# Gate rows through device memory, and the first expert's rows gathered by selection products

## What is computed

```python
sh1, sc1, gt1, sh2, sc2, gt2 = _adaln(cond, w_mod[l], b_mod[l])     # per layer and group
x = x + gt1 * mix(_modulate(x, norm_g[l, 0], sh1, sc1))             # gate 0 (layer 0), gate 2 (layer 1)
h = _modulate(x, norm_g[l, 1], sh2, sc2)
x = x + gt2 * channel_mixer(h)                                      # gate 1 (layer 0), gate 3 (layer 1)
# channel mixer of layer 0: (silu(h @ wg) * (h @ wu)) @ wd, D_FF = 3584
# channel mixer of layer 1:
top_v, top_i = lax.top_k(h @ w_router, 2)
gates = sum(one_hot(top_i) * softmax(top_v))
for e in range(8):
    out = out + gates[..., e:e+1] * _swiglu(h, w_gate[e], w_up[e], w_down[e])
```

## Time and profile before

| | us |
|---|---|
| median of 3 runs (lowest, highest) | 1557.11 (1556.25, 1558.7) |
| profiled execution, its own time | 1554.79 |
| profiled execution, span from first to last instruction | 1553.0 |
| PE busy | 1435.9 (92%) |
| DVE, ACT, POOL busy | 341.5, 313.6, 114.0 |
| mean granted PE clock, of full speed | 0.966 |
| moved by DMA | 497.66 MB, mean 320 GB/s |

### The profile page before, as it was taken

How to read it: one execution, slowest core, us unless ns; L and a number is a source line. 1 busy time by engine, 2 the same in 40 slices (tenths; PEclk the granted TensorE clock), 3 DMA queues, 4 the chain that set the end, 5 groups by cost and what they waited for, 6 DMA issues and landing times.

```text
span 1553.0 us, 27293 instructions
## 1 busy us (share of the span) xinstructions
PE 1435.9 (92%) x12271; PEld 747.2 (48%) x12271; DVE 341.5 (22%) x413; ACT 313.6 (20%) x386; POOL 114.0 (7%) x171
## 2 busy tenths in 40 slices
PE   4998879989999997699999999999999999999963
PEld 1995659767888864233333333333233333333321
DVE  1434782555454444000000000000000000000004
ACT  2435324353343433001000000000000000000001
POOL 4001153341000002000000000000000000000010
PEclk9899989999999998799999999999999999999997
DMA  8757768645555539577999999999999999999994
GB/s 341 247 193 281 271 254 342 229 138 164 190 189 188 189 126 423 208 266 287 352 365 423 424 407 394 382 354 424 423 402 425 422 397 423 424 398 423 423 422 184
DMA packets 124366, 497.66 MB, mean 320 GB/s; under 512 B 10564, under 2 KB 14336, under 8 KB 102752
## 3 DMA queue, kind: packets, MB, share of 16 engines
q1 hardware_dynamic: 110608, 472.51, 77.8%
q10 hardware_dynamic: 12208, 18.26, 3.2%
q0 software_dynamic: 1440, 5.24, 0.9%
HBM read 476.19 MB, written 19.79 MB: 319 GB/s over the span
## 4 chain that ended last, share of the span: by engine, by line
PE 81%; DMA 6%; DVE 4%; SPq 4%; issue 3%; ACT 1%; POOL 0%; ACTq 0%; POOLq 0%; DVEq 0%
PE ps L1951 32%; PE ps L1999 14%; PE ps L368 6%; PE ps L370 6%; PE ps L369 6%; PE ps L1513 4%; DMA ring_a<-in_moe_down 3%; SPq L492 2%; PE ps L1994 2%; PE ps L1715 1%; PE ps L1581 1%; PE ps L1582 1%; PE ps L1583 1%; PE ps L1726 1%; DMA rows_io<-htok,slot 1%
## 5 line engine op out<-in xcount | busy, mean ns | idle before, releaser
L1951 PE MATMUL ps<-ring_a,hTf 128*32 128x512 f32 (+1 forms) x2336 | 230.7, 546 | 3.5 <-DMA ring_a<-in_moe_up 2.1
L1478 DVE TENSOR_TENSOR diag<-gate_bc,ps 128x512 f32<-128x512 f32 (+1 forms) x46 | 28.5, 621 | 875.3 <-PE ps L1951 873.8
L1951 PE MATMUL ps<-raw,hTf 128*32 128x512 f32 (+1 forms) x2080 | 202.8, 541 | 3.8 <-DMA raw<-in_moe_up 3.2
L340 DVE TENSOR_TENSOR w_lo<-raw,w_hi 128x2048 fp32r<-128x2048 f32 x60 | 137.3, 2301 | 155.7 <-ACT w_hi L336 155.7
L1951 PE MATMUL ps<-ring_b,hTf 128*32 128x512 f32 (+1 forms) x1472 | 145.2, 540 | 2.4 <-DMA ring_b<-in_moe_up 2.4
L1951 PEld LDWEIGHTS ps<-ring_a,hTf 128*32 128x32 f32 x2336 | 73.8, 110 | 144.6 <-issue 136.2
L336 ACT ACTIVATE w_hi<-raw 128x2048 fp32r<-128x2048 f32 x60 | 114.0, 1913 | 124.2 <-PE ps L370 124.2
L1951 PEld LDWEIGHTS ps<-raw,hTf 128*32 128x32 f32 x2080 | 65.9, 110 | 125.3 <-issue 118.6
L368 PE MATMUL ps<-w_hi,hTh 128*128 128x512 f32 x288 | 114.9, 399 | 7.9 <-ACT gate_bc L915 5.6
L370 PE MATMUL ps<-w_lo,hTh 128*128 128x512 f32 x288 | 113.6, 394 | 0.0
L369 PE MATMUL ps<-w_hi,hTl 128*128 128x512 f32 x288 | 113.4, 394 | 0.0
(11 more groups left out here) (340 smaller groups left out, 1569.5 us busy)
## 6 DMA issues: line engine op xcount, KB each, us to landing
raw<-in_w_mod SPq DMA_DIRECT2D x48, 1024.0 KB, 7.6
raw<-in_moe_down SPq DMA_DIRECT2D x23, 2048.0 KB, 25.6
ring_a<-in_moe_down SPq DMA_DIRECT2D x19, 2048.0 KB, 23.5
ring_a<-in_moe_gate SPq DMA_DIRECT2D x14, 2048.0 KB, 21.1
ring_b<-in_moe_down SPq DMA_DIRECT2D x14, 2048.0 KB, 24.8
raw<-in_moe_up SPq DMA_DIRECT2D x12, 2048.0 KB, 23.7
ring_a<-in_moe_up SPq DMA_DIRECT2D x12, 2048.0 KB, 24.0
raw<-in_moe_gate SPq DMA_DIRECT2D x10, 2048.0 KB, 14.6
```

The lines of the kernel that those rows point to most:

```text
L340: nc.vector.tensor_tensor(w_lo[:, w % SPLIT], raw[:, slot % RAW], w_hi[:, w % SPLIT].bitcast(F32), ALU.subtract).then_inc(s["lo_ready"], 1)
L1951: last = MM(ps[TOK * j:TOK * j + TOK, part % 4, 0:w], hTf1[:, kt, q * P + TOK * g:q * P + TOK * g + TOK], wt[:, kt % 2, j, :], start=kt == ...
```

## The change

It does two things.

First, the gates. PE turns the gate columns of `mcol` (or `pgate`) into eight rows of 128 (`turn_gates`, two turns for a gate), ACT copies them to a small tile `grow` (`save_gates`), POOL stores them to device memory (`gate_rows`, `store_gates`), waits until they have landed, and then loads each gate row back with every partition reading the same 4 KB (`fetch_gate`: two transfers of 512 KB for each gate). DVE now waits for the landing (`gate_a`, `gate_b`) where it waited for ACT's copy. The products with ones, the `diag` tiles and the big copies are gone.

Second, the first expert. DVE builds for each group a selection matrix, `sel[token, place] = 1` where the token's place in expert 0's list is `place` (`select`). PE multiplies `htok` with it (`gather`: 16 products of 128 x 128), which leaves the gathered rows already turned; ACT copies them as before (`save_rows`). The load of these rows, and the wait of SP for the scatter in front of it, are gone; the scatter itself stays, and SP waits for it in front of the second expert's rows. `gather(p + 1)`, `select` and `save_rows(p + 1, 0)` for a next pass are at the end of each pass and run in the only pass too. `save_tokens(1)` moves ahead of the exponential. The early picks go to two halves of a ring buffer, the late ones to `tmp` and `xrow`.

The diff, without the list of semaphores, paddings and the waits that only follow from them:

```diff
...
+gate_rows = nc.dram_tensor("gate_rows", (4, NB, D), F32, kind="Internal").ap()
...
+grow = sbuf(tail, "grow", [4, P])
...
-diag = sbuf(tail, "diag", [4, 4, P])
-iota = sbuf(tail, "iota", [N_EXP])
+hm = sbuf(tail, "hm", [4, 512])
+iota = sbuf(tail, "iota", [P])
...
+sel = sbuf(tail, "sel", [NB, P])
...
-picked = (htok, spare[:, 0:2])
-late = (spare[:, 2], spare[:, 3])
+picked = (spare[:, 0:2], spare[:, 2:4])
+late = (flat2(tmp), xrow[:, :])
...
-        if p == 0 and i == 0:
+        if p == 0 and i == 1:
             sp.wait_ge(s["rows_sent"], 64)
-        else:
-            sp.wait_ge(s["xg_turned"], N_EXP * p + i)
+        sp.wait_ge(s["xg_turned"], N_EXP * p + i)
...
             ff_loads(p, i, "U0", e)
-            if i == 0:
-                row_load(p, 0, e)
             ff_loads(p, i, "G1", e)
...
-    def gates(i):
-        if i == 0:
-            pool.wait_ge(s["vnew_turned"], 4)
-        else:
-            pool.wait_ge(s["gates_turned"], i + 1)
-        if i == 2:
-            pool.wait_ge(s["pgate_ready"], 1)
-        else:
-            pool.wait_ge(s["mod_cols_saved"], (2, 3, 4, 6)[i])
-        gate = pgate if i == 2 else mcol[:, i // 2, 24 * (i % 2) + 16:24 * (i % 2) + 24]
-        for h in range(2):
-            for b in range(NB):
-                nc.gpsimd.tensor_tensor(diag[:, 2 * h + b], rep(ident[:, :], 1, 4),
-                                        rep(gate[:, 4 * h:4 * h + 4, b], 2, P), ALU.mult)\
-                    .then_inc(s["diag_ready"], 1)
-    gates(0)
+    def store_gates(n, first, count):
+        pool.wait_ge(s["gate_rows_saved"], n)
+        cut = slice(2 * (first % 2), 2 * (first % 2) + 2 * count)
+        pool.dma_start(gate_rows[first:first + count].rearrange("i b (t p) -> t (i b) p", p=P), grow[0:KT, cut])\
+            .then_inc(s["gate_rows_stored"], 16)
+        pool.wait_ge(s["gate_rows_stored"], 16 * n)
+    def fetch_gate(i):
+        for b in range(NB):
+            pool.dma_start(gate_bc[:, i % 2, b], gate_rows[i, b].partition_broadcast(P))\
+                .then_inc(s["gate_b" if i % 2 else "gate_a"], 16)
+    store_gates(1, 0, 2)
+    pool.wait_ge(s["qs_turned"], 1)
+    fetch_gate(0)
+    pool.wait_ge(s["rows_cleared"], 16)
+    fetch_gate(1)
     pool.wait_ge(s["y_turned"], 2)
     nc.gpsimd.memset(w_rt[:, :, :], 0.0).then_inc(s["band_ready"], 1)
-    gates(1)
...
-    nc.gpsimd.iota(iota[:, :], pattern=[[1, N_EXP]], base=0, channel_multiplier=0,
+    nc.gpsimd.iota(iota[:, :], pattern=[[1, P]], base=0, channel_multiplier=0,
...
-    gates(2)
-    gates(3)
+    store_gates(2, 2, 1)
+    pool.wait_ge(s["x_updated"], 2)
+    fetch_gate(2)
...
                                          htok[:, b], None).then_inc(s["rows_sent"], 16)
+    store_gates(3, 3, 1)
+    pool.wait_ge(s["x_updated"], 4)
+    fetch_gate(3)
...
+    def save_gates(n, bank, first, count):
+        act.wait_ge(s["gate_rows_turned"], n)
+        if n > 1:
+            act.wait_ge(s["gate_rows_stored"], 16 * (n - 1))
+        cut = slice(2 * (first % 2), 2 * (first % 2) + 2 * count)
+        nc.scalar.activation(grow[0:KT, cut].rearrange("p a n -> p (a n)"), ps[0:KT, bank, 0:256 * count], ACT.Copy)\
+            .then_inc(s["gate_rows_saved"], 1)
+    save_gates(1, 2, 0, 2)
     act.wait_ge(s["yss_ready"], 1)
-    def save_gate(i, again=0):
-        act.wait_ge(s["gates_turned"], again + i + 2)
-        if i >= 2:
-            act.wait_ge(s["x_updated"], 2 * i - 2)
-        nc.scalar.activation(gate_bc[:, i % 2].rearrange("p b (h n) -> p h b n", n=512),
-                             ps[:, 0:4, :].rearrange("p (h b) n -> p h b n", b=NB), ACT.Copy).then_inc(s["gates_saved"], 1)
     act.wait_ge(s["rows_cleared"], 16)
-    def save_gate0(h):
-        act.wait_ge(s["gates_turned"], h + 1)
-        nc.scalar.activation(gate_bc[:, 0, :, 512 * h:512 * h + 512],
-                             ps[:, 6:8, :], ACT.Copy)\
-            .then_inc(s["gates_saved"], 1)
-    save_gate0(0)
     unit_hi(act, WOUT + 2)
     unit_hi(act, WOUT + 3)
-    save_gate0(1)
     unit_hi(act, FFN)
     modulate(1, 1, hTf1, hTh1)
-    save_gate(1)
...
     ffn_silu(FFN + 1)
+    save_gates(2, 4, 2, 1)
     with act.Fori(1, NC) as cc:
...
     ffn_hidden(NC - 1)
-    save_gate(2)
...
     save_tokens(0)
+    save_tokens(1)
     act.wait_ge(s["mask_ready"], 2)
-    save_tokens(1)
...
-    save_gate(3)
     fetch(finalg[:, :], final_g.partition_broadcast(P), "finalg_loaded")
     act.sem_inc(s["y_saved"], 1)
+    save_gates(3, 3, 3, 1)
+    save_rows(0, 0)
     act.wait_ge(s["route_ready"], 2)
     with act.Fori(0, passes) as p:
-        save_rows(p, 0)
         for i in range(N_EXP):
...
         act.wait_ge(s["rows_stored"], 16 * (STORE_SUM[N_EXP] * p + STORE_SUM[N_EXP]))
+        save_rows(p + 1, 0)
     act.sem_inc(s["rows_done"], 1)
...
-        dve.wait_ge(s["gates_saved"], i + 1 if i == 0 else i + 2)
+        dve.wait_ge(s["gate_b" if i else "gate_a"], 32)
         dve.wait_ge(s["weights_used"], used(i_last))
     def update_second(i, i_last):
-        dve.wait_ge(s["gates_saved"], i + 2)
         dve.wait_ge(s["weights_used"], used(i_last))
...
-    dve.wait_ge(s["gates_saved"], 4)
+    dve.wait_ge(s["gate_a"], 64)
     for b in range(NB):
...
     step(VT(rt[:, 11], ps[:, 1, 0:16].rearrange("p (b e) -> p b e", b=NB), rep(rowbase[:, :], 1, NB), ALU.add))
+    def select():
+        for b in range(NB):
+            nc.vector.tensor_scalar(sel[:, b], iota[:, :], rt[:, 11, b, 0:1], rt[:, 7, b, 0:1], ALU.is_equal, ALU.mult)\
+                .then_inc(s["sel_ready"], 1)
+    select()
     for i in range(2):
...
                 hidden(p, i, c)
-    dve.wait_ge(s["gates_saved"], 5)
+        dve.wait_ge(s["xg_turned"], N_EXP * p + 1)
+        nc.vector.tensor_scalar(rt[:, 11, :, 0:1], rt[:, 11, :, 0:1], float(TOK * POS_G[0]), None, ALU.subtract)\
+            .then_inc(s["sel_ready"], 1)
+        dve.wait_ge(s["sel_ready"], (NB + 1) * p + NB + 1)
+        select()
+    dve.wait_ge(s["gate_b"], 64)
     dve.wait_ge(s["picked"], 64)
...
     last.then_inc(s["state_turned"], 1)
+    def turn_gates(i, bank, at):
+        gate = pgate if i == 2 else mcol[:, i // 2, 24 * (i % 2) + 16:24 * (i % 2) + 24]
+        for b in range(NB):
+            last = turn(ps[0:KT, bank, (at + b) * P:(at + b) * P + P], gate[:, :, b])
+        if i:
+            last.then_inc(s["gate_rows_turned"], 1)
+    turn_gates(0, 2, 0)
+    turn_gates(1, 2, 2)
...
+            pe.wait_ge(s["gate_rows_saved"], 1)
         last.then_inc(s["y_turned"], 1)
-    def gates0(h):
-        for b in range(NB):
-            pe.wait_ge(s["diag_ready"], 2 * h + b + 1)
-            last = MM(ps[:, 6 + b, :], ones[:, :], diag[:, 2 * h + b].rearrange("p a n -> p (a n)"), start=True, stop=True)
-        last.then_inc(s["gates_turned"], 1)
-    def gates(i):
-        for q in range(4):
-            pe.wait_ge(s["diag_ready"], 4 * i + q + 1)
-            last = MM(ps[:, q, :], ones[:, :], diag[:, q].rearrange("p a n -> p (a n)"), start=True, stop=True)
-        last.then_inc(s["gates_turned"], 1)
-    gates0(0)
-        if n == WOUT + 1:
-            pe.wait_ge(s["gates_saved"], 1)
-            gates0(1)
-        if n == WOUT + 2:
-            pe.wait_ge(s["gates_saved"], 2)
-    gates(1)
     turn_xn(1, 1, xn1)
...
-    pe.wait_ge(s["gates_saved"], 3)
     turn_ffn_hidden(0)
+    pe.wait_ge(s["pgate_ready"], 1)
+    turn_gates(2, 4, 0)
         ffn_product(m + 2, 6, 1)
+        if start:
+            pe.wait_ge(s["gate_rows_saved"], 2)
         ffn_down_proj(m + 4, 8, start=start)
...
     pe.wait_ge(s["hc_lo"], NB * NC)
-    gates(2)
     ffn_down_proj(MOE - 2, 4, stop=True)
-    pe.wait_ge(s["gates_saved"], 4)
...
-        pe.wait_ge(s["xrow_loaded"], 16 * (N_EXP * p + i + 1))
-        pe.wait_ge(s["hc_hi"], hbase + PASS_CHUNKS * p + (chunk_at(i - 1, 1, 0) if i else 0))
+        pe.wait_ge(s["xrow_loaded"], 16 * ((N_EXP - 1) * p + i))
+        pe.wait_ge(s["hc_hi"], hbase + PASS_CHUNKS * p + chunk_at(i - 1, 1, 0))
             last = turn(ps[:, 6 + t // 4, (t % 4) * P:(t % 4 + 1) * P], xrow[:, t * P:t * P + P])
+        last.then_inc(s["xg_turned"], 1)
+    def gather(p):
+        pe.wait_ge(s["sel_ready"], (NB + 1) * p + NB)
+        pe.wait_ge(s["hc_hi"], hbase + PASS_CHUNKS * p)
+        for t in range(KT):
+            for b in range(NB):
+                last = MM(ps[:, 6 + t // 4, (t % 4) * P:(t % 4 + 1) * P], htok[:, b, t * P:t * P + P], sel[:, b],
+                          start=b == 0, stop=b == NB - 1)
         last.then_inc(s["xg_turned"], 1)
...
+    pe.wait_ge(s["mod_cols_saved"], 6)
+    turn_gates(3, 3, 0)
+    pe.wait_ge(s["tokens_saved"], 2)
+    gather(0)
     pe.wait_ge(s["route_ready"], 2)
-    gates(3)
     passes = nc.tensor.value_load(npass[0:1, 0:1], min_val=1, max_val=3)
-    pe.wait_ge(s["gates_saved"], 5)
     with pe.Fori(0, passes) as p:
-        turn_rows(p, 0)
         pe.wait_ge(s["xg_hi"], N_EXP * p + 1)
...
         down_product(p, N_EXP - 1, 1)
```

(27 more changed lines are left out.)

4 lines of the change are left out of this document (removed).

## The result

| us | before | changed |
|---|---|---|
| median of 4 runs (lowest, highest) | 1556.68 (1555.76, 1558.7) | 1532.05 (1528.97, 1539.04) |
| profiled execution, span | 1554.79, 1553.0 | 1530.31, 1528.6 |
| PE busy, mean granted clock | 1435.9, 0.966 | 1424.8, 0.975 |

A forecast was written before the change was run, and what follows sets the result against it. In the long expert stage PE and the weight stream were both near their end, with PE's start held by the first expert's rows. Terms summed to -31.0 us: 1523.8 profiled, 1526.1 median; range 1521 to 1540.

The forecast's parts named there:

- Start of the experts: First expert: scatter, load and turns leave the chain for two selections and 16 products; PE starts at 614.9, 23.7 us earlier.
- Clock at the start: First expert's products: coming out of the gather, PE starts them at the higher clock; 2.0 us more gained, 0 at least.
- The stream keeps up: Expert weight transfers: 46 us of slack cover the 25.7 us earlier start, so the whole shift reaches the end.
- Rival B: Weight stream holds the end: only its 14 us pause before the experts is won; -18.0 us, 1539.1; chance 0.09.
- Gate 0: Before the output projection: second product pair leaves the chain, -1.72 us; four turns add 0.25; first pair counted as 0.
- Landing: Gate 0's row, stored and loaded back, lands between 298 and 309, wanted at 306.3; cost 0, or +3 at 309.
- Rival C: Gate 0's way through full queues: it lands at 330.1, 22.1 us late; about +21 us, 1578; chance 0.03.
- Gate 1: Norm's turns before the dense stage: PE begins 3.0 us sooner, but turns run at lower clock; -1.5 us net.
- Gate 2: Dense stage: four products leave the chain, -3.70 us, and only two turns take their place, +0.25 us.
- Tail: After the last expert: ACT's extra copy for a next pass lies on the path to the late picks, +1.05 us.
- Rival A: Gather before the first expert runs at the lower clock, taking 7.0 us, and experts start cold; 1534.1; chance 0.15.
- Rival D: Experts' start still waits for the scatter through a misread semaphore; only the gates' gain remains, 1552; chance 0.03.

The follow-up runs named there:

- again: The same changed kernel measured once more, with no edit, 5 runs: 1526.95 us, ratio 0.9828 to the kernel before.
- best: Changed kernel with gate 2 turned earlier by PE, unread filler products in PE's pauses, and ACT's last copy ahead of its store wait: 1518.84 us, ratio 0.9792.
- order01: Changed kernel with gate 1's two transfers issued ahead of gate 0's: 1527.27 us, ratio 0.9827 to the kernel before.
- load12: Changed kernel plus one unneeded 12.4 MB weight transfer, issued by POOL behind gate 3's when the experts have begun: 1534.38 us, ratio 0.9875.

## Why the prediction was right, and where not

The mechanism was right, one step failed, and two were mis-sized (the clock at gate 0, and the tail). Its steps, by the table:

- **Start of the experts**, -23.7: measured 30.12 - 6.46 = 23.7 in six of the eight profiles with a gather (6.43 to 6.54), 23.0 in the other two (7.15 and 7.19). There PE's signal of the last gather product comes 0.72 and 0.77 us behind that product's record (614.24 behind 613.52 in the first profile, clock 1.00), in again, best and order01 at most 0.04 us, and ACT starts 0.02 us behind the signal in each. So the delay is on PE's side (the ends of its records are modelled) and not ACT's; its cause stays open. The two selections took 0.60 us of the 0.66 forecast, the gather 3.81 of 3.84 (the sum 609.7 + 3.84 is 613.5, not 613.6).
- **Clock at the start**, -2.0: measured 1.83.
- **The stream keeps up:** yes. The shift reaches the last expert whole up to 0.3 us, and load12 puts the slack that is left at an estimated 21 us. Rival B is out: the slack behind the start is there.
- **Gate 0**, -1.72 + 0.25: the product went, but the output projection gained 0.18, since its first products run at 0.62 and 0.52; where the clock held, it gained 1.77. I had looked for this at gate 1 and not at gate 0, whose first pair I called covered at no cost. It was the cover of the clock. The four turns cost nothing (22.38 us from the products near 272 to the output projection, 22.39 before). Landing: its two transfers are issued at 293.91 and 294.49 and land at 300.95 and 304.17: inside 298 to 309, and 5.7 us before their use. Rival C did not come about. Its condition, a landing behind the use, was not met in any run; order01 came within 2.4 us of it at no price.
- **Gate 1**, -1.5: measured -1.83, and 0.34 in the dense units behind it. The turns ran at the lower level as forecast. One forecast sign failed: the first dense product stands at 330.97, not near 327. Of that, 2.05 us are the front's and 1.3 the clock's at gate 0, and the forecast's own steps put it at 328.
- **Gate 2**, -3.70 + 0.25: this is the step that failed. The products are gone (21.17 to 17.73, -3.44), but "nothing takes their place but two turns inside the dense stage" left out ACT: its copy of the turned gate stands in front of the rounding of the next units. 3.26 + 0.44 = 3.7 us, all of the gain. I had listed what the turns cost PE, not what is queued behind the copy that waits for them.
- **Tail**, +1.05: mis-sized. The copy overlaps POOL's start, as the counterpart of the earlier trace rows shows:

```profile
1508.50 0.60 ACT L1024 ACTIVATE yrow<-ps 128x512 f32<-128x512 f32 x1 [13.92 <-PE ps L2015]
1512.50 1.02 ACT L997 ACTIVATE hTf<-ps 128x1024 f32<-128x1024 f32 x1 [3.40 <-DMA rows_io<-yrow]
1513.18 0.94 POOL L715 DMA_INDIRECT tmp<-rows_io,kept  x1 [33.58 <-ACTq L1068]
```

POOL picks 0.68 us after ACT's start, where it was 0.21 before (1537.38 and 1537.59): +0.5 here, +0.36 in the table. The last down product starts 0.36 later, too; why, no run shows.

**Rival A**, the cold gather: no. The gather's records take 3.81 us at clock 1.00, though the clock had been 0.50 at 602 to 604 in the changed kernel's first profile. The Trainium skill ("TensorE: Matmul & The Clock Gate", HAM oscillation) says that waits between bursts bring half rate: the traces agree at the norm's turns and mostly at the output projection, not at the gather. **Rival D**: no. PE's first expert product, at 615.54, is 17 us ahead of the landing of this run's own scatter, at 632.72.

The transfers of the gates, issued at 288.05 and from 293.91 on (tile or tensor, queue, count, KB, median us to landing, 7.0 to 12.5 for the four):

```profile
gate_bc<-gate_rows POOLq DMA_DIRECT2D x4, 512.0 KB, 10.3
...
gate_rows<-grow POOLq DMA_DIRECT2D x1, 16.0 KB, 5.6
```

The Trainium skill ("DMA: Bandwidth & Descriptors", Anatomy of one DMA) gave 3.2 us by estimate for a transfer of 512 KB, a third of the 10.3 measured here with the engines full; the 9.0 us of the earlier trace rows was the nearer price.

**In sum:** behind the front the kernel won 26.5 and 28.3 us of 31.0. 3.7 us are missing at gate 2, 1.3 at gate 0 (none in again), 0.7 in the pause behind the gather (none in again), 0.2 in the clock at the start; gate 1 with the dense units gave 0.7 more than forecast, the tail cost 0.3 less, and another 0.3 came among the experts. The other 2 us between 26.5 and the profile's 24.4 are the front's 2.05, which again did not have. So two single profiles can lie 2 us off what the change does.

## What to carry to other kernels

When a step moves, follow every engine that handles it: a copy of 0.4 us that waits for another engine costs what is queued behind it, not its own time. Products in a pause are not free to remove where their end keeps TensorE at its higher clock: look at the clock behind each, and fill the pause or accept the loss. Here a scatter of 17.8 us and a load on the chain were replaced by 4 us of products on data already in the core, and the gain reached the end whole, because the weight stream in front of it stood still and had slack behind it; count that slack first.
